# Forgetting scores in two rounded passes of 128 stacked rows, the gate's sums among the second pass's rows

## The reference

```
x = x + 0.5 * swiglu(rmsnorm(x), w_ffn1)
proj = rmsnorm(x) @ w_in          # rq rk rv rg | fq fk fv ff | gate_r gate_f
ret  = retention(rope(rq), rope(rk), rv)                # 4 heads of 128
log_f = log_sigmoid(ff + b_forget)                      # 8 heads, (8, 512)
c = cumsum(log_f, over tokens)
logits[t, s] = fq[t] . fk[s] / 8 + c[t] - c[s]          # 8 heads of 64
fox  = softmax(where(s <= t, logits, -1e30)) @ fv
x = x + (sigmoid(gate_r) * ((silu(rg) * norm(ret)) @ w_o_ret)
         + sigmoid(gate_f) * (fox @ w_o_fox)) @ w_out
x = x + 0.5 * swiglu(rmsnorm(x), w_ffn2)
```

## Time and profile before

| | |
|---|---|
| median of 3 runs | 2958.34 us (2954.74 to 2960.34) |
| the profiled execution | 2962.62 us, of which the span is 2960.8 us |
| TensorE busy | 2898.9 us, 98% of the span |
| VectorE busy | 1432.9 us, 48% |
| ScalarE busy | 987.5 us, 33% |
| mean granted TensorE clock | 0.99 |
| memory read | 249.69 MB, 85 GB/s over the span |
| forgetting stage, first layer | about 570 to 676 us of the span |

### The profile page before, as it was taken

One profiled execution on the slowest core, in us unless ns is written; L12 is line 12 of the kernel. 1 busy time (PEld: TensorE's weight loads), 2 busy tenths in 40 slices (PEclk: granted clock), 3 DMA queues, 4 the chain that ended last, 5 costly groups with the idle time before them and its releaser, 6 DMA issues.

```text
span 2960.8 us, 36690 instructions
## 1 busy us (share of the span) xinstructions
PE 2898.9 (98%) x13420; PEld 2377.1 (80%) x13420; DVE 1432.9 (48%) x2066; ACT 987.5 (33%) x1547; POOL 0.2 (0%) x4
## 2 busy tenths in 40 slices
PE   8999999999999999999999999999999999999998
PEld 6888888778888887888887878888887777787777
DVE  6443345554554425444254555544434554455545
ACT  3222223333232222223123333332222344544354
POOL 0000000000000000000000000000000000000000
PEclk9999999999999999999999999999999999899999
DMA  4223232212233332333332212233232221032112
GB/s 142 92 93 107 86 117 79 71 43 93 86 101 98 99 102 79 105 99 96 103 117 72 84 45 71 93 100 99 92 104 87 72 64 51 30 98 87 45 50 72
DMA packets 69223, 253.23 MB, mean 86 GB/s; under 512 B 7680, under 2 KB 7808, under 8 KB 68864
## 3 DMA queue, kind: packets, MB, share of 16 engines
q1 hardware_dynamic: 67824, 246.45, 26.1%
q10 hardware_dynamic: 1296, 5.37, 0.5%
HBM read 249.69 MB, written 2.10 MB: 85 GB/s over the span
## 4 chain that ended last, share of the span: by engine, by line
PE 94%; DVE 3%; ACT 2%; issue 1%; DMA 0%; DVEq 0%; SPq 0%; ACTq 0%
PE bank L495 25%; PE bank L497 25%; PE bank L496 25%; PE bank L658 1%; PE bank L603 1%; PE bank L668 1%; PE bank L605 1%; PE bank L604 1%; PE bank L1050 1%; PE bank L1051 1%; PE bank L1052 1%; PE bank L848 1%; PE bank L859 1%; PE bank L834 1%; PE bank L725 1%
## 5 line engine op out<-in xcount | busy, mean ns | idle before, releaser
L495 PE MATMUL bank<-xh,wh 128*128 128x512 f32 x2384 | 942.6, 395 | 16.9 <-DVE start_d L2276 10.0
L497 PE MATMUL bank<-xh,wl 128*128 128x512 f32 x2384 | 931.5, 391 | 0.0
L496 PE MATMUL bank<-xl,wh 128*128 128x512 f32 x2384 | 931.4, 391 | 0.0
L1612 DVE TENSOR_TENSOR wl<-raw,wh 128x1024 fp32r<-128x1024 f32 x460 | 561.0, 1221 | 321.8 <-ACT wh L1162 320.8
L1162 ACT ACTIVATE wh<-raw 128x1024 fp32r<-128x1024 f32 x460 | 482.8, 1051 | 412.7 <-PE bank L497 248.2
L495 PEld LDWEIGHTS bank<-xh,wh 128*128 128x128 f32 x2384 | 449.9, 189 | 114.7 <-issue 19.1
L497 PEld LDWEIGHTS bank<-xh,wl 128*128 128x128 f32 x2384 | 449.5, 189 | 94.9
L496 PEld LDWEIGHTS bank<-xl,wh 128*128 128x128 f32 x2384 | 450.0, 189 | 92.7 <-issue 1.7
L496 PE MATMUL bank<-ul,wh 128*128 (+1 forms) x704 | 273.9, 389 | 0.0
L495 PE MATMUL bank<-uh,wh 128*128 (+1 forms) x704 | 273.9, 389 | 0.0
L497 PE MATMUL bank<-uh,wl 128*128 (+1 forms) x704 | 273.9, 389 | 0.0
(11 more groups left out here) (380 smaller groups left out, 2831.0 us busy)
## 6 DMA issues: line engine op xcount, KB each, us to landing
raw<-stream SPq DMA_DIRECT2D x460, 512.0 KB, 3.5
x<-x_t SPq DMA_DIRECT2D x4, 512.0 KB, 8.1
dec<-decay ACTq DMA_DIRECT2D x2, 1024.0 KB, 6.2
out<-x SPq DMA_DIRECT2D x4, 512.0 KB, 2.6
rp<-rope ACTq DMA_DIRECT2D x2, 512.0 KB, 7.0
g_post<-rows ACTq DMA_DIRECT2D x2, 512.0 KB, 3.3
cst<-const SPq DMA_DIRECT2D x1, 708.5 KB, 10.4
ffraw<-ff_w ACTq DMA_DIRECT2D x2, 316.0 KB, 10.0
```

What stands on the lines that cost most here:

```text
L495: pe.matmul(o, wh[:, s, c], rhs_h, start=first, stop=False)
L496: pe.matmul(o, wh[:, s, c], rhs_l, start=False, stop=False)
L497: return pe.matmul(o, wl[:, s, c], rhs_h, start=False, stop=last)
L1612: dve.tensor_tensor(wl[:, at.slot, :], raw[:, at.raw, :], wh[:, at.slot, :].bitcast(F32), ALU.subtract).then_inc(split_lo, 1)
```

## The change

The one fp32 product of a score tile becomes two rounded ones. Queries and keys are taken out of their banks whole (`q32`, `k32`, VectorE), ScalarE rounds them by half-height copies, VectorE subtracts the rounded from the whole to get the rests. Pass one multiplies `qhh` (rounded queries on both halves of the rows) with `khl` (rounded keys on one half, their rests on the other); pass two multiplies `qlc` (rests of the queries, and -8) with `kgh` (rounded keys, and the gate's sums). The sums are now split too, into rounded and rest in two groups of eight rows, so the gate's weights stand four times in a strip of 104 rows (856 columns). A pass has at least 256 columns; the tiles have new places in the banks for that.

The order changes in three places. TensorE takes values of head 1 before the next scores of head 0. VectorE's `fox_load` is split into queries, sums, keys and rests with waits for ScalarE between them, the normalising of head 1 and a `low` are moved ahead of the next maxima. ScalarE gets four half-height copies for queries behind its second `high`, and four for keys behind its turned pieces of head 1.

```diff
             def fox_scores(it, e):
                 for qt in range(TT):
-                    b, c = HEAD_AT[qt]
+                    b, c = FOX_AT[qt]            # ((3, 256), (3, 0), (2, 0), (4, 0))
                     n = (qt + 1) * P
-                    pe.matmul(bank[b][:, c:c + n], fq[:, e, qt * P:n], fk[:, e, 0:n], start=True, stop=False)
+                    cols = max(n, 2 * P)
+                    pe.matmul(bank[b][:, c:c + cols], qhh[:, e, qt * P:n], khl[:, e, 0:cols], start=True, stop=False)
+                    pe.matmul(bank[b][:, c:c + cols], qlc[:, e, qt * P:n], kgh[:, e, 0:cols], start=False, stop=False)
                     last = pe.matmul(bank[b][:, c + n - P:c + n], ident16[:], causal, start=False, stop=True)
...
                     transposes(fp[:, 0, :], fx_t[0].sem)
+                    pe.wait_ge(*fx_q.at(it, "KLB"))
+                    pe.wait_ge(*fx_r.at(it, "GB"))
                     fox_scores(it, 1)
...
                     transposes(fp[:, 1, :], fx_t[1].sem)
+                    fox_values(it, 1, v)
                     if not last_pair:
-                        pe.wait_ge(*fx_q.at(it + 1, "KB"))
+                        pe.wait_ge(*fx_q.at(it + 1, "KLA"))
+                        pe.wait_ge(*fx_r.at(it + 1, "GA"))
                         fox_scores(it + 1, 0)
-                    fox_values(it, 1, v)
...
+            def fox_queries(it):                                   # ScalarE
+                act.wait_ge(*fx_q.at(it, "Q"))
+                for shift in range(2):
+                    for e in range(2):
+                        act.activation(qhh[HALVES[e ^ shift], e, :], q32[HALVES[e], :], ACT.Copy).then_inc(fx_r.sem, 1)
+            def fox_keys(it, e):
+                act.wait_ge(*fx_q.at(it, "K"))
+                for dst in khl, kgh:
+                    act.activation(dst[HALVES[e], e, :], k32[HALVES[e], :], ACT.Copy).then_inc(fx_r.sem, 1)
...
                     fox_probs(it, 1)
                     high(at + 1 + LEAD)
+                    if not last_pair:
+                        fox_queries(it + 1)
                     fox_turned(it, 1, first)
                     if not last_pair:
+                        fox_keys(it + 1, 0)
+                        fox_keys(it + 1, 1)
                         fox_probs(it + 1, 0)
...
                 high(idx + LEAD)
+                fox_queries(l * pairs)
                 high(idx + 1 + LEAD)
+                fox_keys(l * pairs, 0)
+                fox_keys(l * pairs, 1)
                 fox_probs(l * pairs, 0)
...
+            def fox_queries(it, at):                               # VectorE
+                dve.wait_ge(panel_done, at.done())
+                dve.tensor_tensor(q32, bank[0][:], rstd[:], ALU.mult).then_inc(fx_q.sem, 1)
+                for e in range(2):
+                    dve.wait_ge(*fx_r.at(it, ("QA", "QB")[e]))
+                    dve.tensor_tensor(qlc[HALVES[e], e, :], q32[HALVES[e], :], qhh[HALVES[e], e, :].bitcast(F32),
+                                      ALU.subtract).then_inc(fx_q.sem, 1)
+            def fox_keys(it, at):
+                dve.wait_ge(panel_done, at.done())
+                dve.tensor_tensor(k32, bank[1][:], rstd[:], ALU.mult).then_inc(fx_q.sem, 1)
+            def fox_keys_low(it, e):
+                dve.wait_ge(*fx_r.at(it, ("KA", "KB")[e]))
+                dve.tensor_tensor(khl[HALVES[1 - e], e, :], k32[HALVES[e], :], khl[HALVES[e], e, :].bitcast(F32),
+                                  ALU.subtract).then_inc(fx_q.sem, 1)
...
-                        fox_load(it + 1, t2 + 1, idx + (t2 * 2 + 2))
+                        at = idx + (t2 * 2 + 2)
+                        fox_queries(it + 1, at)
+                        low(at + LEAD)
+                        fox_sums(it + 1, t2 + 1)
+                        fox_keys(it + 1, at + 1)
                     fox_turned(it, 1, first)
                     if not last_pair:
+                        fox_keys_low(it + 1, 0)
+                        fox_keys_low(it + 1, 1)
+                    fox_normed(it, 1)
+                    if not last_pair:
+                        low(at + 1 + LEAD)
                         fox_max(it + 1, 0)
-                    fox_normed(it, 1)
...
-                fox_load(l * pairs, 0, idx)
+                fox_queries(l * pairs, idx)
+                low(idx + LEAD)
+                fox_sums(l * pairs, 0)
+                fox_keys(l * pairs, idx + 1)
+                fox_keys_low(l * pairs, 0)
+                fox_keys_low(l * pairs, 1)
+                low(idx + 1 + LEAD)
                 fox_max(l * pairs, 0)
...
                 dve.wait_ge(*ffs.at(l, "C"))
-                for e, rows in enumerate((slice(FDH, P), slice(0, FDH))):
-                    dve.memset(fq[rows, e, :], -FDH ** 0.5).then_inc(fx_set, 1)
-                    dve.memset(fk[rows, e, :], 0.0).then_inc(fx_set, 1)
+                dve.tensor_copy(kgh[0:FF_W, 0, :], cum[0:FF_W, :]).then_inc(ffs.sem, 1)
+                dve.wait_ge(*ffs.at(l, "CH"))
+                for half in HALVES:
+                    rows = slice(half.start + FF_LOW, half.start + FF_LOW + FH)
+                    dve.tensor_tensor(cum[rows, :], cum[rows, :], kgh[rows, 0, :].bitcast(F32), ALU.subtract)\
+                       .then_inc(ffs.sem, 1)
+                dve.wait_ge(*ffs.at(l, "CL1"))
+                for e, half in enumerate(HALVES[::-1]):
+                    dve.memset(qlc[half, e, :].bitcast(F32), -FDH ** 0.5).then_inc(fx_set, 1)
+                    dve.memset(kgh[half, e, :].bitcast(F32), 0.0).then_inc(fx_set, 1)
```

More of the change, by code:

```diff
@@ L29 @@
 FH, FDH = 8, 64
-FF_W = FDH + FH
+FF_LOW = 32
+FF_W = FDH + FF_LOW + FH
 FF_COLS = KD * FF_W + P - FF_W
+GATE_ROWS = (0, FF_LOW, FDH, FDH + FF_LOW)
 MH, M_NOPE, M_ROPE, M_V, QR, KVR = 4, 64, 32, 64, 256, 128
@@ L216, in build @@
         fq = sb("fq", [P, 2, S], F32, heads)
-        fk = sb("fk", [P, 2, S], F32, heads)
+        kgh = sb("kgh", [P, 2, S], F32R, heads)
+        gap("qlc", 256, heads)
+        qlc = sb("qlc", [P, 2, S], F32R, heads)
         ff_mem = ExitStack()
@@ L245, in build @@
         finv = sb("finv", [P, 2, TT], F32, fox_mem)
+        gap("khl", 128, fox_mem)
+        khl = sb("khl", [P, 2, S], F32R, fox_mem)
+        gap("qhh", 256, fox_mem)
+        qhh = sb("qhh", [P, 2, S], F32R, fox_mem)
         fox_mem.close()
+        q32, k32 = fq[:, 0, :], fq[:, 1, :]
         fz, fa = fq[:, 0, :], fq[:, 1, :]
@@ L356, in build @@
         tm = Steps(sem("tm_dve"), *[f"RV{i}" for i in range(TT)], *[f"FV{i}" for i in range(TT)])
-        ffs = Steps(sem("forget_dve"), "H", "L", "Z", "ZB", "LF", "C")
+        ffs = Steps(sem("forget_dve"), "H", "L", "Z", "ZB", "LF", "C", "CH", "CL0", "CL1")
         ffs_pe = Steps(sem("forget_pe"), "FF")
@@ L373, in build @@
         fx_y = Steps(sem("fox_out_pe"), "TR")
-        fx_q = Steps(sem("fox_qk_dve"), "CA", "CB", "QA", "QB", "KA", "KB")
+        fx_q = Steps(sem("fox_qk_dve"), "Q", "QLA", "QLB", "CA", "CB", "K", "KLA", "KLB")
+        fx_r = Steps(sem("fox_qk_act"), "QA", "QB", "RA", "RB", "KA", "GA", "KB", "GB")
         fx_m = [Steps(sem(f"fox_max_{e}_dve"), "M", "N") for e in "ab"]
@@ L438, in build @@
         HEAD_AT = ((2, 0), (3, 0), (2, 128), (4, 0))
+        FOX_AT = ((3, 256), (3, 0), (2, 0), (4, 0))
+        HALVES = (slice(0, FDH), slice(FDH, P))
         HEAD_OUT = 2 * P
@@ L712, in forgetting @@
                 pe.wait_ge(*ret_y.at(l * RH + RH - 1, "Y"))
-                pe.wait_ge(*fx_q.at(l * pairs, "KB"))
+                pe.wait_ge(*fx_q.at(l * pairs, "KLA"))
+                pe.wait_ge(*fx_r.at(l * pairs, "GA"))
                 pe.wait_ge(mask_set, 2)
@@ L1234, in fox_probs @@
                 for qt in range(TT):
-                    b, c = HEAD_AT[qt]
+                    b, c = FOX_AT[qt]
                     n = (qt + 1) * P
@@ L1762, in retention, with fox_sums @@
                 ret_norm(l * RH + RH - 1)
-            def fox_load(it, t2, at):
-                for e, rows in enumerate((slice(FDH, FF_W), slice(0, FH))):
-                    dve.tensor_scalar(fk[rows, e, :], cum[rows, :], cst[rows, t2 * 2 + C_HOT + e:t2 * 2 + C_HOT + e + 1],
+            def fox_sums(it, t2):
+                for e, rows in enumerate((slice(FDH, FF_W), slice(0, FF_LOW + FH))):
+                    dve.tensor_scalar(kgh[rows, e, :], cum[rows, :], cst[rows, t2 * 2 + C_HOT + e:t2 * 2 + C_HOT + e + 1],
                                       None, ALU.mult).then_inc(fx_q.sem, 1)
[L1769 to L1775, removed]
+            def fox_queries(it, at):
[12 more added lines that the diff above has]
+                                  ALU.subtract).then_inc(fx_q.sem, 1)
             def fox_max(it, e):
@@ L2385, in table_of_constants @@
     c[96:96 + half, C_FREQ] = freqs
-    c[0:FH, C_HOT:C_HOT + FH] = c[FDH:FF_W, C_HOT:C_HOT + FH] = np.eye(FH)
+    for r in GATE_ROWS:
+        c[r:r + FH, C_HOT:C_HOT + FH] = np.eye(FH)
     return c
@@ L2498 @@
```

(6 more changed lines are left out.)

## The result

Median of six timed runs 2977.85 us (2967.91 to 2981.5), beside six of the kernel before at 2958.89 (2954.74 to 2963.86): ratio 1.0056, 95% interval 1.0035 to 1.0077. Forecast were 2971 us, 2958 to 2980, slower with a chance of 0.74. The profiled execution took 2977.95 us, span 2976.0, mean granted clock 0.986; before it was 2960.8 at 0.99.

A forecast was written before the change was run, and what follows sets the result against it. TensorE was taken to bound the kernel, with 94% of the chain of waits. +2.4 us at full clock and +10.2 for clock falls gave +12.6 us, carried to the median of 2958.34: 2971 us, range 2958 to 2980.

The forecast's parts named there:

- score set: Forgetting stage, sixteen sets: rounded products cut a set from 2.55 to 1.7 us, saving 13.6 us at full clock.
- gap at a pair's end: TensorE waits for VectorE's late copy of turned weights: 0.41 to 1.8 us; six pairs net -1.2 us.
- gap at the start of the stage: First forgetting scores wait for a longer VectorE and ScalarE chain, +1.9 us each; net +1.5 us for two.
- gap ahead of retention: VectorE's added copy and two subtractions delay retention's first scores, 0.35 to 2.15 us; +3.6 us for two.
- full clock, sum: Whole kernel without clock losses: -1.2 - 1.5 + 1.5 + 3.6 = +2.4 us.
- the clock: Half-clock stretches after the new TensorE gaps: six falls of 1.7 us, +10.2 us.
- four falls in the six: Six new 1.8 us gaps at pairs' ends: four followed by a clock fall costing 1.7 us each.
- have their falls already: The two gaps at the start of the forgetting stage: clock already falls there, so no further loss counted.
- rival (c): Later half-height copies or 256-column products costing 0.23: all eight gaps fall, +23 us, 2981 us; chance 0.11.
- Rival (a): New gaps come but the clock holds in nearly all, at most one fall: 2961 to 2962.5 us; chance 0.20.
- Rival (b): VectorE's small operations from SBUF cost near 0.4 us, not 0.69: -4.2 us, 2954 us; chance 0.06.
- the rule weighed there: Skill warns of idle gaps longer than any of the eight new ones; by it alone nothing falls, +2.4 us.

The follow-up runs named there:

- split alone: Kernel before plus one copy of 72 rows and two subtractions of 8 rows between scan and memsets, results unused: 2968.94 us, ratio 1.004.
- with fill: Throw-away TensorE products in gaps: of the changed kernel 2968.35 us, of the kernel before 2964.01 us, of all repairs 2946.45 us.
- late split: Changed kernel with the split of the gate's sums and the memsets moved behind retention's first head: 2977.64 us, ratio 1.0067; run again 2974.51 us, ratio 1.0052.
- order: Changed kernel with VectorE's sums made inside the wait for ScalarE's rounding and the low half behind the key rests: 2961.41 us, ratio 1.001.
- all repairs: Changed kernel with order and late split, and keys ahead of low half and panel rounding at the start of the stage: 2952.05 us, ratio 0.9976.
- narrow products: All repairs without fill, the first tile's products at 128 columns instead of 256: 2945.97 us, ratio 0.9945.

## Why the prediction was right, and which term was too small

| step | forecast | measured |
|---|---|---|
| score set | 1.7 us, saves 0.85 | 1.82, saves 0.73 |
| gap at a pair's end, six | 0.41 to 1.8 | 1.81 to 1.84 |
| gap at the start of the stage, two | 1.91 to 3.8 | 4.01, 4.04 |
| gap ahead of retention, two | 0.35 to 2.15 | 2.46, 2.43 (split alone: 2.42) |
| full clock, sum | +2.4 | +2.3 ± 1.6 |
| the clock | +10.2 | +14.0 ± 4.5 (the two profiles: +12.6) |
| all | +12.6 | +16.4 ± 5.1 by means, +19 by medians |

- **End of a pair.** Right in place, releaser and size. The counted queue of VectorE behind its wait for the rounded queries gave 1.8; taking two pieces out of it gave 0.72 and 6.9 us of full part.
- **Score set.** The slope by columns held (0.12 for 256), the price of changing tiles was put a little low. It is 0.12 a set, 2 us in all.
- **Ahead of retention.** The right mechanism, priced low: the gap grew by 2.1, not 1.8, in the changed kernel and with the split alone, and the split alone costs +4.3 at full clock for the forecast's 3.6. 0.43 and 1.40 are the durations that had been put at 0.42 and 1.30; the rest is the steps between them.
- **The full sum** agrees so well partly by luck: set, start and retention were each put low, by 16 x 0.12, 2 x 0.2 and 2 x 0.3, 2.9 us together, and that is not in the measured sum. Part of it is how the sum is measured: the idle time booked to the clock is 1.1 us in the profile where 2 x 0.3 had been allowed for it, and behind 2280 it is 0.6 more than in the kernel before. What else came out cheaper, some 1.8 us, the interval of 1.6 doesn't let one say.
- **The clock.** The step that was off is "I take four falls in the six and both of the two: 6 x 1.7 = 10.2 us", and that the starts "have their falls already". Five came, not six, but the last two pairs of layer 1 took 3.4 each, and both starts of the stage, which the forecast left out because they had their falls already, went from 1.7 to 3.4. In the profiled execution: 1.7 x 3 + 3.4 x 2 + 1.7 x 2 = 15.3, less 2.8 elsewhere, some 13; over the timed runs 14.0, whose interval of 4.5 holds the forecast's 10.2 too. That these gaps cause the falls is shown by filling them. That their number came out near is partly luck: four falls in the six was a guess between a gap of 1.6 us that held and gaps of 1.9 that mostly didn't, and it was three, all in one layer.
- **The time.** 2977.85 lies in the stated range, but just above the forecast's own 2964 to 2977 and nearer to rival (c)'s 2981 than to 2971. By means, 16.4 stands nearer to the forecast's 12.6 than to (c)'s 23.
- **Rival (a)**, the clock holds, is out: 1.8 us gaps were followed by falls in three of six cases. **Rival (b)**, cheap VectorE operations, is out: 0.70 each. **Rival (c)** is out by its premises: gaps of 1.8, 0.12 for 256 columns. It would have been wrong too in letting all eight gaps fall: five did.
- By the rule weighed there, of the Trainium skill, "TensorE: Matmul & The Clock Gate", Part 1 (HAM oscillation), none of the eight new gaps is long enough to matter. The traces disagree: 0.50 of the clock after 1.83 and 2.46 us.

**Open**: why equal gaps differ, why what the clock takes after 2280, where no kernel differs, is anything from 11.7 to 33.1 us in the eleven profiles (the highest two with fill, but 17.7 with fill too), and why a fall takes 1.7 us here and 3.4 there. No experiment took this apart.

## What to carry to other kernels

Split each timed run into span times clock and the rest: the first tells, averaged over six runs or more, what an edit is worth to a microsecond or two, the second is most of the run-to-run spread and is judged over many runs alone. When products get cheaper by splitting operands, count what the splitting puts in the queue of the engine that also releases TensorE; here 16 sets gave 12 us, and three operations in a wrong place, one order of a queue and a longer start of the stage took all of it and more, until they were moved. Put what isn't yet due (low halves, rests of later operands) behind what TensorE waits for, and do it before trusting any saving.

## What the runs showed of the hardware

- A gap of 1.8 us in dense work can halve the clock, with a loss of 1.7 or 3.4 us, while of the 24 gaps of 0.7 at pairs' ends in the profiles of four kernels (order, all repairs, those with fill, narrow products) two were followed by a fall, 2.4 and 2.5 us behind the gap with TensorE busy between. Which gaps of 1.8 it strikes went by layer: three of three in layer 1 of the changed kernel and none in layer 2, the other way round with the late split, where two profiles gave the same pattern.
- What the clock takes in one and the same code differs widely: after 2280 us 11.7 to 33.1 us in eleven profiles. Filling two gaps in the kernel before removed 3.4 us of falls there and didn't lower what the clock took on average (+3.0 ± 3.5).
- Half-height copies on ScalarE (64 x 512) take 2.60 / 4 = 0.65 us each; a subtraction of 8 x 512 on VectorE takes 0.70 (1.40 / 2), as one of 64 x 512 does (1.41 / 2), and one of 128 x 1024 takes 1.23: rows don't matter, columns do.
